# Hybrid attention and gMLP step on eight cores: attention outputs transposed by the loads, first output sums as filler, a finer ramp

## The chip, the cores and the metric

The kernel runs on all 8 cores of one Trainium2 chip, one launch per execution. The time is the device time of the slowest core, in microseconds. Even cores (0, 2, 4, 6) have role 0, odd cores role 1; each pair works on one of four sequences. The two roles run different programs that one function, `emit(ctx, role)`, writes out.

## The reference, cut to what matters

One layer on 4 prompts of 4096 frames and 8 running streams of 16 frames, model width 2048:

```python
h = rmsnorm(x, norm_g)
z = h @ w_in            # columns: q | k | v | f | g_A | u | v_B | g_B
out_a = fox_attention(q, k, v, logf) * silu(g_a)       # 8 heads of 128, causal
out_b = gmlp_mix(gelu(u), layernorm(gelu(v_b))) * silu(g_b)   # 8 groups of 128
y = rmsnorm(x + concat([out_a, out_b]) @ w_out, final_g)
```

The results are y, the keys, the values and the log forget gates, for prompts and streams, and the normalised gMLP rows of the streams.

## The kernel before, in words

A core keeps its normalised input H in SBUF in bf16, channels on partitions, and walks through five stages. Role 0 owns blocks 0 to 19 of its sequence (a block is 128 frames). Role 1 owns blocks 20 to 31 and one stream block of 32 rows, and computes K and V of blocks 0 to 19 for itself once more.

1. **Ramp** (to about 100 us). A *unit* is a pair of blocks. For each unit `n` the list `ramp` (L535) names the steps: `G` scales the unit's x by the norm's gains into H (VectorE and ScalarE, L390 and L392), `S` squares (ScalarE L400, GpSimd L401), `T` ends the tree of sums (VectorE L408, L409), `R` lets TensorE add over the partitions and ScalarE make 1/rms (L420 to L423), `X m` loads the x of unit m, and `K n q` multiplies the unit with the key weights of heads 2q and 2q+1 (`k_mm`) into one PSUM bank; `k_out` (L460) evacuates a bank when its unit has its `R`. The weights `wk`, one tile a head, come over GpSimd's DMA queue, the first three units of x over SP's. The order of the list is the order on every engine.
2. **V, layer norm of gMLP** and the rest of K (to about 460 us).
3. **gMLP** (to about 750 us): `c_chunk` and `mixing`; its products go to the scratch tensor `oT_s`, rows 8 to 15, channels first.
4. **Attention** (about 750 to 1236 us). Heads one after another; in a head the query tiles T (512 queries) from the last to the first; in a tile one *unit* per block of keys: `e_S(i)` is one 128x512 score matmul, then an exp on ScalarE (L1117), a mask on GpSimd on the diagonal (L1120); `e_PV(i-3)` multiplies three units later with V (up to four matmuls of 129 columns). Role 0 has 60 units a head, 480 in all. After a tile's last unit `fin` (L1173, L1176) divides by the sum and multiplies with the gate, into a tile `og`, queries on partitions. Three units later `tr` (L1189 to L1194) lets TensorE transpose it (four transposes of 128x128 into the bank `ob`, L1190), VectorE copies it (L1192), and SP stores it to `oT_s`.
   Between the units TensorE gets *filler*: `qga(h)` computes the queries (`q_item`) and gates (`g_item`, L977 to L984) of the coming tiles. Each step of a generator yields its cost in ns; `due` lists by which unit how much must be done; `fill(i)` raises its target by the steepest of these demands and steps until it is reached. The last demand is everything by unit 474. An item's last step counts 56 whatever it is.
   `wo_load` brings the 16 tiles of `w_out` over GpSimd's queue as memory comes free, mostly in head 7. `o_load` brings a group of four output blocks (16 tiles of 128 KB) from `oT_s` to SBUF over SP's queue.
5. **Output** (about 1236 us to the end). For each of the 20 blocks 64 matmuls of 512 columns (16 channel tiles k times four column groups cg) into four PSUM banks, the order of k in `korder` = 8 to 15, 0 to 7; VectorE adds x (L1332), ScalarE sums squares, VectorE scales (L1340), SP stores y. At each fourth block `o_load` fetches the group after. The last block goes cg by cg, with short evacuations (L1305 to L1325) and four stores.

```python
def fill(i):
    while due and due[0][1] <= filler["target"]:
        due.pop(0)
    if due:
        filler["target"] += max((c - filler["target"]) / max(at - i, 1) for at, c in due)
    ...
    while filler["gen"] is not None and filler["done"] < filler["target"] and ...:
        step()

def icost(it):
    return (tilesP[it[1]][1] / 2.4 + 3) * KC if it[0] == "q" else 56 * KC * (4 if it[1] < NT else 1)
```

Of the kernel before, what the change touches and what calls it, by code (L numbers as in the profile page):

```python
# [51 lines left out]
class Eng:  # L52
# [156 lines left out]
def build_program(only_role=None):  # L209
# [8 lines left out]
    def dscr(name, shape, dt=BF16):  # L218
# [18 lines left out]
        oT_s=dscr("oT_s", [KC, 128, N_HEAD_BLOCKS * 128]))  # L237
# [24 lines left out]
def emit(ctx, role):  # L262
# [28 lines left out]
    def load(q, out, in_, res, part=False, reads=()):  # L291
        q.dma(out, in_, dsem(res.name + "_p") if q is POOL else dsem_of(res), reads=reads, writes=[] if part else [res], pwrites=[res] if part else [])
# [86 lines left out]
    def g_mul(n):  # L379
# [4 lines left out]
        for a0, cnt in ([(0, 1), (1, 1)] if n == 0 else [(0, na)]):  # L384
# [52 lines left out]
    def k_mm(n, heads):  # L437
        u = units_n[n]
        hv, rh = h_of(n)
        bank, w, rows = next_bank(), u["w"], u["rows"]  # L440
        parts = [(a, 1) for a in range(u["na"])] if n == 0 and heads[0] == 0 else [(0, u["na"])]
        for a, cnt in parts:
            for hi_, h in enumerate(heads):
                o = hi_ * w + a * rows
                for k in range(KC):
                    mmop(PSB[bank][:, o:o + cnt * rows], WK[h][:, k, :], hv[:, k, a * rows:(a + cnt) * rows], k == 0, k == KC - 1,
                         rh[a:a + cnt] + [WK[h].r], bank, k == 0 and o == 0, k == KC - 1 and hi_ == len(heads) - 1 and a + cnt == u["na"])
        return n, heads, bank
# [81 lines left out]
    for h in range(2, 8):  # L530
# [4 lines left out]
    ramp = [("G", 0), ("S", 0), ("K", 0, 0), ("T", 0), ("G", 1), ("S", 1), ("X", 3), ("K", 0, 1), ("K", 1, 0), ("R", 0), ("K", 1, 1),  # L535
# [3 lines left out]
    normed, wait = set(), []  # L539
    for e in ramp:  # L540
        what, n = e[:2]
        if what == "G":
            g_mul(n)
# [14 lines left out]
        elif what == "X":  # L558
            x_load(n)
        elif what == "R":  # L560
            rms(n)
            normed.add(n)
        else:
            wait.append(k_mm(n, [2 * e[2], 2 * e[2] + 1]))
# [205 lines left out]
    def cum_gen():  # L770
# [7 lines left out]
        nbt = A.alloc("nbt", [3, 256], F32)  # L778
# [117 lines left out]
    def mixing(gi, ti):  # L896
# [20 lines left out]
        store(SP, io["oT_s"][8 + gi, :, c0:c0 + n], o[:, 0:n], o.r, R_oT[8 + gi][ti])  # L917
# [9 lines left out]
    A.free(*(Ub + Gb + t1))  # L927
# [12 lines left out]
    for T in torder:  # L940
        items += [("q", ti) for ti in TQ[T][::-1] if ("q", ti) not in items] + [("g", T)]
        if smp and T == torder[0]:
            items.append(("g", NT))

# [69 lines left out]
    while (0, "g", torder[0]) not in done:  # L1014
        next(lead)
# [5 lines left out]
    og = [A.alloc("og%d" % i, [4, 128], BF16, hi=True) for i in range(2)]  # L1021
# [22 lines left out]
    def wo_load(n):  # L1044
        for _ in range(n):
            k = wo_next["k"]
            if k >= KC or not A.gaps(D * 2):
                return
            wo[k] = A.alloc("wo%d" % k, [D], BF16)
            load(POOL, wo[k][:, :], io["wout"][k], wo[k].r)  # L1050
            wo_next["k"] += 1

    oT, xr, fgt = [], [], []
# [5 lines left out]
    def o_load(gp, ks):  # L1059
        if gp < len(fgroups):  # L1060
# [3 lines left out]
            for k in ks:  # L1064
                t.res[k].dsem = dsem("oTg%d%s" % (gp % 2, "ab"[k == 7]))
                load(SP, t[:, k, 0:n], io["oT_s"][k, :, c0:c0 + n], t.res[k], reads=[R_oT[k][gi]])
# [32 lines left out]
    pending = []  # L1099
# [62 lines left out]
    def fin(i):  # L1162
# [3 lines left out]
        z = u["tid"] % 2  # L1166
        o, rc = og[z], rec[z]
        need((h, "g", T))
        s = ost[u["tid"] % 3]
        if u["kind"] == "blk":  # L1170
# [9 lines left out]
            nq, rows, c0, n = 4, 128, T * 512, 512  # L1180
        else:
# [43 lines left out]
    due.append((len(units) - 6, cum))  # L1225
# [209 lines left out]
```

How the kernel before makes its waits and increments, by code:

```python
    def _wait(self, ev):  # L60
        sem, val = ev
        if sem is self.sem and self.is_pe:
            return
        if self.seen.get(id(sem), 0) >= val:
            return
        self.eng.wait_ge(sem, val)
        self.seen[id(sem)] = val
# [34 lines left out]
    def op(self, fn, reads=(), writes=(), pwrites=(), sig=True):  # L102
        self._deps(reads, writes, pwrites)
        ins = fn()
        if sig:
            ins.then_inc(self.sem, 1)
            self.cnt += 1
            ev = (self.sem, self.cnt)
        else:
            ev = (self.sem, self.cnt + 1)
        self._update(ev, reads, writes, pwrites)
        return ev
# [1 line left out]
    def dma(self, out, in_, dsem, reads=(), writes=(), pwrites=()):  # L114
        self._deps(reads, writes, pwrites)
        self.eng.dma_start(out=out, in_=in_).then_inc(dsem.sem, 16)
        dsem.cnt += 16
        ev = (dsem.sem, dsem.cnt)
        self._update(ev, reads, writes, pwrites)
        return ev
```

The softmax here doesn't subtract the row's maximum and nothing guards it: scores larger than these inputs give would overflow.

## Time and profile before

| | us |
|---|---|
| median of 3 runs (lowest, highest) | 1529.27 (1529.13, 1530.7) |
| the profiled execution | 1526.34 |
| its span, even cores (role 0) | 1522.6 |
| its spans, odd cores (role 1) | 1500.7 to 1502.7 |
| TensorE busy on core 0 | 1478.3 |
| VectorE, ScalarE, GpSimd busy | 582.1, 608.4, 155.0 |

The span runs from the first to the last instruction of the slowest core; the execution's own time is 3.7 us more. A busy TensorE means that some matmul was in flight, not that it ran at its peak. All times within the span below are of core 0, role 0.

### The profile page before, as it was taken

Reading aid. Unit: us, or ns where it says so; the run is one execution under the profiler, and the core shown is the slowest. Engines: PE = TensorE matmul, PEld = TensorE weight load, DVE = VectorE, ACT = ScalarE, POOL = GpSimd, SP = SyncE. Lnnn points to the kernel's source line nnn. Section 1 sums busy time; section 2 is a strip of 40 time slices with the busy share of each in tenths; the row PEclk is TensorE's granted clock in tenths of the full one; section 3 lists DMA queues with packets and bytes.
Section 4 is the critical chain, followed back from the end, with each engine's and each line's share of the span. In section 5 each row is a group of like instructions: output and inputs, shape, how many; then the busy total and the mean of one; then the engine's idle time right before and its main releaser. Section 6 shows DMA issues by size and latency. Waiting matters only on the chain.

```text
span 1522.6 us, 30070 instructions; the slowest of 8 cores (1500.7 to 1522.6 us)
## 1 busy us (share of the span) xinstructions
PE 1478.3 (97%) x11216; PEld 907.6 (60%) x11216; DVE 582.1 (38%) x1143; ACT 608.4 (40%) x1051; POOL 155.0 (10%) x279
## 2 busy tenths in 40 slices
PE   4999999999999999999999999999999989999997
PEld 3886877854444444444577767777777754444443
DVE  2340222214455655555523333233233333333334
ACT  3322423136662111111366666666666641111112
POOL 4310111210000000000002111112011200000000
PEclk9999999999999999999999999999999999999999
DMA  9993335750003222222516245133340975654643
GB/s 248 241 242 106 128 132 148 164 142 1 1 1 59 48 58 49 49 45 46 81 20 90 40 74 78 37 50 53 45 63 12 191 196 165 201 195 159 221 147 132
DMA packets 86886, 158.13 MB, mean 104 GB/s; under 512 B 28368, under 2 KB 68944, under 8 KB 78544
## 3 DMA queue, kind: packets, MB, share of 16 engines
q0 software_dynamic: 34096, 48.53, 20.9%
q1 hardware_dynamic: 50624, 92.91, 18.4%
q10 hardware_dynamic: 2016, 14.68, 2.8%
q8 instruction: 94, 1.54, 0.4%
q14 instruction: 56, 0.46, 0.1%
HBM read 152.12 MB, written 52.51 MB: 134 GB/s over the span
## 4 chain that ended last, share of the span: by engine, by line
PE 95%; DMA 2%; DVE 1%; issue 1%; ACT 1%; POOL 0%; POOLq 0%; DVEq 0%; ACTq 0%
PE psb L304 94%; DMA arena<-wk 2%; PE psb L1190 1%; DVE arena L1176 0%; ACT arena L1117 0%; POOL arena L116 0%; DVE arena L977 0%; DVE arena L982 0%; POOLq L253 0%; ACT arena L981 0%; DVE arena L1173 0%; DVE arena L1192 0%; ACT arena L1319 0%; ACT arena L1307 0%; DVE arena L1305 0%
## 5 line engine op out<-in xcount | busy, mean ns | idle before, releaser
L304 PE MATMUL psb<-arena 128*128 128x512 bf16 (+5 forms) x11056 | 1475.0, 296 | 33.4 <-DMA arena<-wk 24.3
L304 PEld LDWEIGHTS psb<-arena 128*128 128x128 bf16 x11056 | 900.1, 99 | 602.9 <-issue 50.7
L1117 ACT ACTIVATE arena<-psb,arena 128x512 bf16<-128x512 f32 x480 | 298.8, 632 | 133.9 <-PE psb L304 127.5
L1337 ACT ACTIVATE arena<-arena 128x2048 bf16<-128x2048 f32 x19 | 36.3, 1910 | 224.7 <-DVE arena L1332 224.7
L874 DVE TENSOR_TENSOR arena<-psb,arena 128x512 f32<-128x512 f32 x80 | 55.2, 691 | 97.5 <-PE psb L304 96.0
L1332 DVE TENSOR_TENSOR arena<-psb,arena 128x512 f32<-128x512 f32 x76 | 47.2, 682 | 109.8 <-PE psb L304 109.8
L1120 POOL TENSOR_SCALAR_AFFINE_SELECT arena<-arena 128x128 bf16<-128x128 bf16 x160 | 49.1, 308 | 360.1 <-ACT arena L1117 359.7
L497 ACT ACTIVATE arena<-psb,arena 128x384 f32<-128x384 f32 (+1 forms) x60 | 30.3, 544 | 121.3 <-PE psb L304 106.7
L977 DVE TENSOR_TENSOR arena<-psb,arena 128x512 f32<-128x512 f32 x40 | 27.6, 691 | 120.5 <-PE psb L304 120.5
L891 ACT ACTIVATE arena<-arena 128x512 f32<-128x512 f32 x40 | 25.2, 631 | 117.3 <-DVE arena L874 114.5
L887 ACT ACTIVATE arena<-arena 128x512 bf16<-128x512 f32 x40 | 25.1, 629 | 107.8 <-DVE arena L874 107.7
L401 POOL TENSOR_TENSOR arena<-arena 128x1024 f32<-128x1024 f32 x20 | 46.6, 2352 | 209.4 <-ACT arena L400 209.4
L460 DVE TENSOR_TENSOR arena<-psb,arena 128x512 f32<-128x512 f32 x40 | 26.5, 688 | 101.6 <-PE psb L304 50.6
L1176 DVE SCALAR_TENSOR_TENSOR arena<-psb,arena 128x128 bf16<-128x128 f32 x160 | 56.0, 350 | 17.7 <-DVE arena L1173 1.3
L956 DVE TENSOR_TENSOR arena<-psb,arena 128x512 bf16<-128x512 f32 x40 | 27.6, 689 | 81.4 <-PE psb L304 81.4
L400 ACT ACTIVATE arena<-arena 128x2048 f32<-128x2048 f32 x20 | 37.1, 1901 | 40.7 <-DVE arena L390 40.7
L484 DVE SCALAR_TENSOR_TENSOR arena<-psb,arena 128x8 f32<-128x8 f32 x20 | 4.5, 225 | 114.9 <-PE psb L304 114.9
L1340 DVE SCALAR_TENSOR_TENSOR arena<-arena 128x2048 f32<-128x2048 f32 x19 | 44.7, 2351 | 2.4 <-DVE arena L1339 0.6
L982 DVE SCALAR_TENSOR_TENSOR arena<-arena 128x512 bf16<-128x512 f32 x40 | 27.7, 692 | 33.3 <-ACT arena L981 33.3
L981 ACT ACTIVATE arena<-arena 128x512 f32<-128x512 f32 x40 | 25.2, 630 | 33.3 <-DVE arena L977 33.3
L1192 DVE COPY arena<-psb 128x512 bf16<-128x512 bf16 x40 | 17.0, 424 | 50.9 <-PE psb L1190 48.5
L723 ACT ACTIVATE arena<-psb,arena 128x512 f32<-128x512 f32 x40 | 27.1, 683 | 20.0 <-PE psb L304 18.5
(81 smaller groups left out, 468.6 us busy)
## 6 DMA issues: line engine op xcount, KB each, us to landing
arena<-xn SPq DMA_DIRECT2D x20, 1024.0 KB, 7.3
y<-arena SPq DMA_DIRECT2D x19, 1024.0 KB, 4.8
arena<-xT ACTq DMA_DIRECT2D x14, 1024.0 KB, 10.2
kT<-arena SPq DMA_DIRECT2D x40, 256.0 KB, 9.8
oT_s<-arena SPq DMA_DIRECT2D x80, 128.0 KB, 1.8
arena<-oT_s SPq DMA_DIRECT2D x80, 128.0 KB, 4.7
arena<-wout POOLq DMA_DIRECT2D x16, 512.0 KB, 22.2
vo<-arena SPq DMA_DIRECT2D x40, 192.0 KB, 2.4
```

The costliest lines, as they stand in the source:

```text
L304: PE.op(lambda: mm(out, lhsT, rhs, start=start, stop=stop, **kw), reads=reads, writes=[PSR[bank]] if first else [], pwrites=[] if first el ...
L400: ACT.op(lambda: act.activation(out=x, in_=x, func=AF.Square), reads=[t.res[a]], writes=[t.res[a]])
L401: POOL.op(lambda: g.tensor_tensor(out=x[:, 0:8, :], in0=x[:, 0:8, :], in1=x[:, 8:16, :], op=ALU.add), reads=[t.res[a]], writes=[t.res[a]])
L497: ACT.op(lambda: act.activation(out=o, in_=src, func=AF.Copy, scale=rc), reads=[PSR[bk[c]], rr], writes=[dst.r] if first else [], pwrites= ...
L874: DVE.op(lambda: v.tensor_tensor(out=z[:, 0:n], in0=PSB[b][:, 0:n], in1=rbw[:, c0:c0 + n], op=ALU.mult), reads=[PSR[b]] + rbw.res, writes= ...
L982: DVE.op(lambda: v.scalar_tensor_tensor(out=GAh[p][0:rows, j0:j0 + cnt, :].rearrange("p j c -> p (j c)"), in0=th[0:rows, 0:n], scalar=1.0, ...
L1117: ACT.op(lambda: act.activation(out=P[:, off:512], in_=PSB[b][:, off:512], func=AF.Exp, scale=SCALE, bias=nb[:, T, j, h:h + 1]), reads=[PS ...
L1120: POOL.op(lambda: g.affine_select(out=P[:, off:off + 128], in_=P[:, off:off + 128], pattern=[[1, 128]], compare_op=ALU.is_ge, fill=0.0, ba ...
L1176: DVE.op(lambda c=c, q=q, ps=ps: v.scalar_tensor_tensor(out=o[:, 2 * c + q, :], in0=ps[:, q, 0:128], scalar=rc[:, 2 * c + q:2 * c + q + 1] ...
L1332: DVE.op(lambda cg=cg, b=b: v.tensor_tensor(out=yb[p][q, cg * 512:(cg + 1) * 512], in0=PSB[b][q, :], in1=xr[p][q, cg * 512:(cg + 1) * 512] ...
L1337: ACT.op(lambda: act.activation(out=junk[q, :], in_=yb[p][q, :], func=AF.Square, accum_out=ss), reads=[yb[p].r], writes=[junk.r, R_ss[p]])
L1340: DVE.op(lambda: v.scalar_tensor_tensor(out=yb[p][q, :], in0=yb[p][q, :], scalar=rs, in1=fgt[0][q, :], op0=ALU.mult, op1=ALU.mult), reads= ...
```

## The change

- **Transposes.** `fin` no longer queues `tr`: it stores the tile as it is, queries first, to a new scratch tensor `o_s` (rows of 128 elements, 256 bytes). `o_load` fetches the eight attention tiles of a group with `dma_start_transpose` on SP, the eight gMLP tiles as before (from `mT_s`). TensorE's transposes, VectorE's copies and the list `pending` are gone; `og` has three buffers.
- **Spread loads.** The gMLP tiles of the first output group are loaded when attention begins, and each head's tile right behind its store.
- **Output sums as filler.** Behind the last `qga` the generator `out_ahead` goes through 15 of the 16 k of the first output block for as many column groups as filler has banks (two in role 0, one in role 1), if the weights are there. They are due by unit 479. The weights come in `korder`, and `ring[0]`, `ring[1]` are freed early in head 7.
- **Order of the filler.** A gate item now stands behind the next tile's query item; the lead before attention computes two query items instead of one query and one gate item.
- **Ramp.** K goes in quarters (one head, one block) where weights arrive; `R` and `G` move ahead of the evacuations; `S` and `X` come later.
- **Last block.** Five column groups, the last two of 256; the first two stores go over ScalarE's queue.

```diff
-    ramp = [("G", 0), ("S", 0), ("K", 0, 0), ("T", 0), ("G", 1), ("S", 1), ("X", 3), ("K", 0, 1), ("K", 1, 0), ("R", 0), ("K", 1, 1),
-            ("T", 1), ("G", 2), ("S", 2), ("X", 4), ("K", 0, 2), ("K", 1, 2), ("K", 2, 0), ("R", 1), ("K", 2, 1), ("K", 2, 2),
-            ("T", 2), ("G", 3), ("S", 3), ("K", 0, 3), ...
+    ramp = [("G", 0, [(0, 1), (1, 1)]), ("S", 0), ("K", 0, 0, [(0, 0, 1)]), ("G", 1, [(0, 1)]), ("T", 0), ("G", 1, [(1, 1)]), ("S", 1), ("X", 3),
+            ("K", 0, 0, [(1, 0, 1), (0, 1, 1), (1, 1, 1)]), ("K", 0, 1, [(0, 0, 2)]), ("K", 1, 0, [(0, 0, 1), (1, 0, 1)]), ("K", 1, 1, [(0, 0, 1)]),
+            ("K", 0, 1, [(1, 0, 2)]), ("K", 1, 1, [(1, 0, 1)]), ("K", 1, 0, [(0, 1, 1), (1, 1, 1)]), ("K", 1, 1, [(0, 1, 1), (1, 1, 1)]),
+            ("T", 1), ("G", 2), ("R", 0), ("K", 0, 2), ("K", 1, 2), ("R", 1), ("S", 2), ("X", 4), ("K", 2, 0), ("K", 2, 1), ("K", 2, 2),
+            ("T", 2), ("G", 3), ("R", 2), ("S", 3), ("K", 0, 3), ...
...
+        if i > 0:
+            items.append(("g", torder[i - 1]))
...
-                load(SP, t[:, k, 0:n], io["oT_s"][k, :, c0:c0 + n], t.res[k], reads=[R_oT[k][gi]])
+                src = io["o_s"][k, c0:c0 + n, :] if k < 8 else io["mT_s"][k - 8, :, c0:c0 + n]
+                load(SP, t[:, k, 0:n], src, t.res[k], reads=[R_oT[k][gi]], tr=k < 8)
...
-        def tr():
-            b = ob
-            for q in range(nq):
-                PE.op(lambda q=q: nc.tensor.transpose(psb16[b][:, q * rows:(q + 1) * rows], o[0:rows, q, :], ident[0:rows, 0:rows]),
-            ...
-            DVE.op(lambda: v.tensor_copy(out=s[:, 0:n], in_=psb16[b][:, 0:n]), reads=[PSR[b]], writes=[s.r])
-            store(SP, io["oT_s"][h, :, c0:c0 + n], s[:, 0:n], s.r, R_oT[h][T])
+            store(SP, io["o_s"][h, T * 512:(T + 1) * 512, :].rearrange("(c q) d -> q c d", c=4), o[:, :, :], o.r, R_oT[h][T])
+        if T == torder[0]:
+            o_load(0, [h])
...
+    def out_ahead():
+        for k in korder[:-1]:
+            if wo[k] is None:
+                return
+            for cg in range(len(fbank["list"])):
+                pre.append((k, cg))
+                mmop(PSB[obank[cg]][:, :], oT[0][:, k, ...], wo[k][:, cg * 512:(cg + 1) * 512], k == korder[0], False, ...)
+                yield 216
...
-    due.append((len(units) - 6, cum))
+    due += [(len(units) - 6, cum), (len(units) - 1, cum + 216 * 15 * len(fbank["list"]))]
...
-                A.free(KTh[0], Vh[0], Qh[0], GAh[0])
+                A.free(KTh[0], Vh[0], Qh[0], GAh[0], ring[0], ring[1])
...
-        kcg = [(k, cg) for cg in range(4) for k in korder] if last else [(k, cg) for k in korder for cg in range(4)]
+        cgs = [(512 * i, 512) for i in range(4)] if not last else [(0, 512), (512, 512), (1024, 512), (1536, 256), (1792, 256)]
+        kcg = [(k, cg) for cg in range(5) for k in korder] if last else [(k, cg) for k in korder for cg in range(4)]
...
-                store(SP, dst[:, c4], yb[p][q, c4], R_q[cg])
+                store(ACT if cg < 2 else SP, dst[:, c4], yb[p][q, c4], R_q[cg])
```

## Rows read from the trace of the kernel before

**Rows 1.** The page: busy time by engine, and the chain that ended last.
```profile
PE 1478.3 (97%) x11216; PEld 907.6 (60%) x11216; DVE 582.1 (38%) x1143; ACT 608.4 (40%) x1051; POOL 155.0 (10%) x279
...
PE 95%; DMA 2%; DVE 1%; issue 1%; ACT 1%; POOL 0%; POOLq 0%; DVEq 0%; ACTq 0%
```
**Rows 2.** Spans of the cores, one of role 1.
```profile
core 1: 1500.7 us, clock 0.995
```
**Rows 3.** Attention as a window: length, busy by engine, granted clock, DMA share, GB/s.
```profile
740.00:1250.00 510.00, 496.35 (x5516) 363.12 (x5611) 174.74 (x413) 322.80 (x524) 77.34 (x204) 1.00 0.42 75
```
**Rows 4.** Waits of TensorE over the span: total us, times, longest.
```profile
PE psb L304 <- DMA arena<-wk: 24.1, 5, 13.1
PE psb L304 <- ACT arena L1117: 4.7, 9, 1.2
PE psb L1190 <- DVE arena L1176: 2.0, 3, 1.1
...
PE psb L304 <- DVE arena L1192: 0.7, 1, 0.7
```
**Rows 5.** Lines by form, the transposes: busy us, mean ns, idle before.
```profile
L1190 PE MATMUL psb<-arena 128*128 128x128 bf16 x160 | 15.4, 219 | 2.0 <-DVE arena L1176 2.0
```
**Rows 6.** Timeline of TensorE around one tile's transposes: start, length.
```profile
793.84 0.39 PE L1190 MATMUL psb<-arena 128*128 128x128 bf16 x4
794.06 11.97 PE L304 MATMUL psb<-arena 128*128 128x128 bf16 x135
```
**Rows 7.** End of attention: last gate (timeline), exps behind it (by line), the window.
```profile
1223.29 0.69 DVE L977 TENSOR_TENSOR arena<-psb,arena 128x512 f32<-128x512 f32 x1 [0.79 <-PE psb L304]
...
L1117 ACT ACTIVATE arena<-psb,arena x18: 367/626/688, 1222.8 to 1234.4; 128x512 bf16<-128x512 f32 x9, 128x384 bf16<-128x384 f32 x3, 128x256 bf16<-128x256 f32 x3, 128x128 bf16<-128x128 f32 x3
...
1223.50:1236.30 12.80, 9.23 (x85) 6.03 (x84) 5.38 (x16) 9.58 (x19) 3.50 (x12) 1.00 0.77 196
```
**Rows 8.** Output weights in head 7, by tile: issues on GpSimd's queue, landing.
```profile
L116 POOL DMA_DIRECT2D arena<-wout x12: 528/558/592, 1186.2 to 1202.5; - x12
...
DMA to landing us min/median/max: 11.6/23.7/29.6
```
**Rows 9.** Last block (timeline), its last stores, and 256-column operations (by line).
```profile
1513.81 0.69 DVE L1305 TENSOR_TENSOR arena<-psb,arena 128x512 f32<-128x512 f32 x1
1514.60 0.63 ACT L1307 ACTIVATE arena<-arena 128x512 bf16<-128x512 f32 x1 [1.68 <-DVE arena L1305]
...
1517.04 2.08 SPq L116 DMA_DIRECT2D y<-arena  x4
...
L409 DVE TENSOR_TENSOR arena<-arena 128x256 f32<-128x256 f32 x10 | 4.3, 425 | 1.0
L422 ACT ACTIVATE arena<-arena 128x256 f32<-128x256 f32 x10 | 4.2, 417 | 0.9
```
**Rows 10.** Ramp: timeline of TensorE, with the idle time before.
```profile
25.00 1.91 PE L304 MATMUL psb<-arena 128*128 128x256 bf16 x16 [1.56 <-DMA arena<-wk]
31.45 13.99 PE L304 MATMUL psb<-arena 128*128 128x256 bf16 x102 [4.53 <-DMA arena<-wk]
46.93 13.29 PE L304 MATMUL psb<-arena 128*128 128x256 bf16 x119 [1.49 <-DMA arena<-wk]
```
**Rows 11.** Ramp as windows, columns as in rows 3.
```profile
31.40:36.00 4.60, 4.55 (x22) 3.20 (x23) 0.00 (x0) 0.31 (x1) 3.30 (x2) 0.50 1.01 274
36.00:45.40 9.40, 9.40 (x82) 8.07 (x80) 3.92 (x7) 3.29 (x9) 0.00 (x0) 0.96 0.98 251
```
**Rows 12.** Output stage: landing of oT_s loads (by tile), two groups' issues, SP's queue.
```profile
DMA to landing us min/median/max: 1.7/4.7/6.9
...
1300.93 10.09 SPq L116 DMA_DIRECT2D arena<-oT_s  x16
...
1356.18 9.82 SPq L116 DMA_DIRECT2D arena<-oT_s  x16
...
q1 hardware_dynamic: 50624, 92.91, 18.4%
```

More of the change, by code:

```diff
@@ L383, in g_mul @@
         hv, rh = h_of(n)
-        for a0, cnt in ([(0, 1), (1, 1)] if n == 0 else [(0, na)]):
+        for a0, cnt in parts or [(0, na)]:
             x, rx, rd = t[:, a0:a0 + cnt, :, 0:rows], t.res[a0:a0 + cnt], rh[a0:a0 + cnt]
@@ L435, in next_bank, with k_mm @@
         return b
-    def k_mm(n, heads):
+    def k_mm(n, heads, rec=None, parts=None):
         u = units_n[n]
         hv, rh = h_of(n)
[L440 to L448, printed above, removed]
+        w, rows = u["w"], u["rows"]
+        new = rec is None
+        rec = rec or (n, heads, next_bank())
+        bank = rec[2]
+        for i, (hi_, a, cnt) in enumerate(parts or [(hi_, 0, u["na"]) for hi_ in range(len(heads))]):
+            o = hi_ * w + a * rows
+            for k in range(KC):
+                mmop(PSB[bank][:, o:o + cnt * rows], WK[heads[hi_]][:, k, :], hv[:, k, a * rows:(a + cnt) * rows], k == 0, k == KC - 1,
+                     rh[a:a + cnt] + [WK[heads[hi_]].r], bank, new and k == 0 and i == 0, k == KC - 1)
+        return rec
     def k_out(rec):
@@ L563, in emit @@
         else:
-            wait.append(k_mm(n, [2 * e[2], 2 * e[2] + 1]))
+            part = e[3] if len(e) > 3 else [(0, 0, 2), (1, 0, 2)]
+            rec, got = count.get((n, e[2]), (None, 0))
+            rec, got = k_mm(n, [2 * e[2], 2 * e[2] + 1], rec, part), got + sum(p[2] for p in part)
+            count[n, e[2]] = rec, got
+            if got == 4:
+                wait.append(rec)
         for r_ in [r_ for r_ in wait if r_[0] in normed]:
@@ L939, in emit @@
     items, done = [], set()
-    for T in torder:
-        items += [("q", ti) for ti in TQ[T][::-1] if ("q", ti) not in items] + [("g", T)]
-        if smp and T == torder[0]:
+    for i, T in enumerate(torder):
+        items += [("q", ti) for ti in TQ[T][::-1] if ("q", ti) not in items]
+        if i > 0:
+            items.append(("g", torder[i - 1]))
+        if smp and i == 1:
             items.append(("g", NT))
+    items.append(("g", torder[-1]))
     def q_item(h, ti):
@@ L1013, in emit @@
     fbank["list"] = [6, 7, (cb["n"] + 2) % 6, (cb["n"] + 3) % 6]
-    while (0, "g", torder[0]) not in done:
+    while (0,) + items[len(TQ[torder[0]])] not in done:
         next(lead)
@@ L1020, in emit @@
     Pb = [A.alloc("Pb%d" % i, [512], BF16, hi=True) for i in range(NP)]
-    og = [A.alloc("og%d" % i, [4, 128], BF16, hi=True) for i in range(2)]
+    og = [A.alloc("og%d" % i, [4, 128], BF16, hi=True) for i in range(3)]
     rec = [A.alloc("rec%d" % i, [4], F32, hi=True) for i in range(2)]
@@ L1045, in wo_load @@
         for _ in range(n):
-            k = wo_next["k"]
-            if k >= KC or not A.gaps(D * 2):
+            if wo_next["k"] >= KC or not A.gaps(D * 2):
                 return
+            k = korder[wo_next["k"]]
             wo[k] = A.alloc("wo%d" % k, [D], BF16)
@@ L1208, in fgen @@
             yield from qga(h)
+        yield from out_ahead()
+    pre = []
+    def out_ahead():
[4 more added lines that the diff above has]
+                pre.append((k, cg))
+                mmop(PSB[obank[cg]][:, :], oT[0][:, k, (border[0] % 4) * 128:(border[0] % 4 + 1) * 128], wo[k][:, cg * 512:(cg + 1) * 512],
+                     k == korder[0], False, [oT[0].res[k], wo[k].r], obank[cg], k == korder[0], True)
+                yield 216
     def icost(it):
@@ L1300, in emit @@
         if last:
-            R_q = [Res("yq%d" % i) for i in range(4)]
-            for cg in range(4):
-                b = 4 * p + cg
-                c4 = slice(cg * 512, (cg + 1) * 512)
-                DVE.op(lambda: v.tensor_tensor(out=yb[p][q, c4], in0=PSB[b][q, :], in1=xr[p][q, c4], op=ALU.add),
+            R_q = [Res("yq%d" % i) for i in range(5)]
+            for cg, (g0, w) in enumerate(cgs):
+                b = obank[(4 * p + cg) % 8]
+                c4 = slice(g0, g0 + w)
+                DVE.op(lambda: v.tensor_tensor(out=yb[p][q, c4], in0=PSB[b][q, 0:w], in1=xr[p][q, c4], op=ALU.add),
                        reads=[PSR[b], xr[p].r], writes=[R_q[cg]] + ([yb[p].r] if cg == 0 else []), pwrites=[] if cg == 0 else [yb[p].r])
```

65 lines of the change are left out of this document (27 added, 38 removed), and 5 rows, old and new, of the table ramp.

## The prediction

> **What bounds the kernel now.** I read the page's busy times and its chain first: TensorE is busy 97% of the span and makes up 95% of the chain [rows 1], VectorE and ScalarE are at 40% and below. Then the cores: role 1 ends 21.9 us before role 0 [rows 2], so the time is role 0's, and nothing that only role 1 gains counts. Then attention: of 510 us TensorE is busy 496.4, ScalarE, which makes the exps, 322.8 [rows 3]. Filler keeps TensorE the bound there. Then TensorE's waits [rows 4]: the large one is for the key weights in the ramp; in attention 4.7 us for exps, 2.0 of the transposes for VectorE's `fin`, 0.7 for the copy of the last tile. The sum is made against the profiled execution, 1526.3 us (span 1522.6 and 3.7 around it); the median of the runs shown, 1529.3, is 2.9 higher, and I move both by the same amount.
>
> **1. Transposes off TensorE.** 160 are removed. They are busy 15.4 us, 219 ns each [rows 5], but they overlap with what follows: four start at 793.84 and the next matmul at 794.06 [rows 6], so a tile costs 0.22 us of TensorE's order and 40 tiles 8.8 us. Above, all 15.4 could count; below, nothing, if ScalarE set the pace, but its 63% in rows 3 excludes that for most tiles. I take 8.8, the start-to-start time, as that is what the next matmul waits. The two waits that hang on them go with them: 2.0 + 0.7 = 2.7 us. The Trainium skill, "TensorE: Matmul & The Clock Gate", section "Part 4: PE-mode transpose", gives about 275 ns for a transpose in a kernel's context; by that the term would be 44 us and the time 1482, but here the trace disagrees: 55 ns from one to the next (as a mechanism of this kernel it is rival F). VectorE's 40 copies cost nothing now and give nothing. What is late next is the transposing load.
>
> **2. The transposing loads.** `fin` stores 128 KB as before, in rows of 256 bytes; nobody waits on TensorE, and the three `og` buffers leave at least two tiles, over 8 units of about a microsecond, to land. SP then waits for that store before it issues the load of the same tile, once a head; behind it stands only the next tile's store, 16 units later. In the output stage a group of 16 loads has the time of four blocks: 1356.18 - 1300.93 = 55.2 us [rows 12]. Plain ones take SP 10 us to issue and land within 1.7 to 6.9, median 4.7. The trace has no transposing load. Below, it lands as the fastest plain one, 1.7 us; above, it moves two bytes at a time: 65,536 pieces at the queue's mean per packet (18.4% of 16 x 1522.6 us over 50,624 packets = 88 ns [rows 12]) on 16 engines, 360 us. I take 5 us, the median's size, because one instruction on the same queue names the whole tile, so it is nearest to that row: eight take 40 us even one behind the other, under 55.2, and are used only in the second half of a block's order of k. While they hold SP, the y store and the x load behind them come up to 40 us late; x is needed two blocks (27.6 us) after, so with 7 us of landing VectorE's addition slips by about (40 + 7) - 41 = 6 us, 8 us ahead of the reuse of its banks. Cost 0; without that cover, 8 us per group for each microsecond above 6.9 a load (rival B). The Trainium skill, "VectorE: DVE Perf Modes", section "The three transpose paths", gives 1309 ns for 128x128 by the DMA crossbar; an estimate from it is 5.2 us a load, 42 a group: by that page this term stays 0 and B falls out. No run here shows it yet.
>
> **3. Output sums as filler.** By the planner's own costs a query item counts (512/2.4 + 3) x 16 = 3.46 us and a gate item 3.58, 281.8 us in all, 274.9 without the lead; what the generators really yield is less, since an item's last step counts 56 ns: 268.5. So filler runs dry early. In the trace the last gate is evacuated at 1223.29, and 18 exps run from then on; in 1223.5 to 1236.3 TensorE is idle 12.80 - 9.23 = 3.57 us [rows 7]. The change adds 15 x 2 matmuls, 6.5 us, due by unit 479: the target now rises by (274.9 + 6.5)/479 = 0.587 us a unit, and 268.8 + 6.5 us last until unit 468, where before they ended at 462. A third of the 18 bare units is covered, so 3.57 x 6/18 = 1.2 us is gained; the matmuls themselves are only moved. Bounds: 0 to 3.57. They need 15 of 16 weight tiles. Of the twelve loaded in head 7, the last lands at up to 1202.5 + 29.6 us [rows 8], and the reordered gates free H some six units later; but two ring buffers come free at once, and 2 MB of output tiles have been loaded before. I take the weights as just in time; the loss if not is a rival.
>
> **4. Tail.** The last sum waits for 256 columns instead of 512: VectorE 0.43 for 0.69, ScalarE 0.42 for 0.63 [rows 9], 0.5 us. Four stores on SP took 2.08 us; with two on ScalarE about 0.5 of that goes. Gain 1.0, bounds 0 and 1.6.
>
> **5. Ramp.** TensorE stands still for weights at 25.00, 31.45 and 46.93, and never after [rows 10]; in this stretch the DMA engines are full (share 0.98 to 1.01 [rows 11]). The fifth tile (head 4) lands at 46.9, and everything behind it waits for it in either order. The quarters fill the gap of 4.5 us before 31.45: 16 matmuls of 256 columns and three sixteens of 128 are 4.8 us from 25.00. Behind 31.45 seven sixteens of 128 columns are left, about 6.5 us, so they end at 38 instead of 45.4. Nothing is won: TensorE now waits 9 us before 46.9 where it waited 1.5. And after such a pause it runs slower: behind the 4.5 us one, 22 matmuls took 4.60 us at a granted clock of 0.50, 1.2 GHz, then 82 took 9.40 at 0.96, close to 2.4 GHz [rows 11]. At the second rate the 22 take 2.5, so the slow start cost 2.1 us, until now in slack. Moved behind 46.9 it is on the path: +2.1. On the other side two stores of keys (0.5 MB, 2 us of the DMA engines at 251 GB/s) leave the window before 46.9, because `R 0` now stands behind `G 2`, which waits for the third x; of that the weights' queue, one of three, gets some 0.6. Net +1.5, bounds -1.5 and +2.3. `S 2`, `X 4` and the value weights are issued some 10 us later, where TensorE has 30 us or more of K before it needs them: 0, and if that cover fails, a wait for x in the fifth unit.
>
> Everything else at 0: the new place of the gates (still due two units before use), the lead (the same 7 us), allocations. **Sum:** -8.8 - 2.7 - 1.2 - 1.0 + 1.5 = -12.2: 1514.1 for the profiled execution, 1517 for the median. Role 1 sheds 104 transposes and stays ahead.
>
> **Rivals.** *A, forecast*: 1517, its own range 1514 to 1521; chance 0.60.
> *B, slower*: the transposing loads set the pace of the output stage. The point is 55.2/8 = 6.9 us a load. At twice the plain median, 9.4, a group takes 75 us, 20 too long, four times: 1517 + 80 = 1597. For it speaks that no row shows such a load; against it that one would have to take longer than the slowest plain one of 64. Chance 0.06.
> *C*: the time freed is not on the path, because units are paced by ScalarE: only the waits, filler and tail count, -2.7 - 1.2 - 1.0 + 1.5 = -3.4, 1526. For it: TensorE's 4.7 us of waits for exps; against it: 63%. Chance 0.09.
> *D*: the fifth weight comes early enough that the clock holds (term 5 at -1.5), and the short gaps around tiles close: 13.65 us of idle in rows 3 less 7.4 named in rows 4 leaves 6, half of it 3. 1517 - 6 = 1511. Chance 0.10.
> *E*: the output weights are late, and TensorE, in order, stands before them with scores queued behind. Two tiles later by six units is 6 us: 1523. For it: landing times of up to 29.6 us; against it: less traffic. Chance 0.10.
> *F*: a transpose costs its whole 219 ns: 160 x 219 ns = 35 us, 26 more: 1491. Rows 6 speak against it. Chance 0.03.
> *G*, the change doesn't do what it says: `out_ahead` returns at once because a weight tile has no room yet; 1518. Chance 0.02.
>
> **The numbers.** A measurement of this kernel tells about 0.2%, 3.1 us, from no change. Faster by more: A, D, E, F, G and half of C, 0.89; within: the rest of C, 0.05; slower: B, 0.06. The range 1511 to 1523 takes in A, D, E and G, 0.82; it leaves out B, C and F.
>
> **What would show it.** No L1190 and L1192; next matmul behind a tile without the 0.22 us; about 12 us less between 750 and 1237. Transposing loads that land in 2 to 6 us and no wait of TensorE for them; one would prove B. In the ramp one wait before the fifth weight of about 9 us at 47, and a granted clock of 0.5 behind it. Thirty matmuls of 512 columns before the last exp, fewer than 18 exps behind the last filler. It is wrong if attention is not some 11 us shorter, or if a new wait stands in the output stage.

## The result and the profile after

The changed kernel takes 1519.39 us (median of 1518.79, 1519.39 and 1523.55; before 1529.27). The ratio is 0.994, 95% interval [0.9912, 0.9969]: faster by 0.6%, and inside the range. A fourth, disturbed execution of 7076.91 us is left out; with it the median is 1521.47, which the expectations below start from. The sum of the parts was -12.2 us; the profiled execution, 1518.79, has -7.5, and the span of its slowest core went from 1522.6 to 1514.3, -8.3.

The page (of core 4, as are the views below unless said otherwise): busy time, and the chain by engine.
```profile
PE 1469.4 (97%) x11136; PEld 902.6 (60%) x11136; DVE 570.1 (38%) x1115; ACT 609.9 (40%) x1059; POOL 153.8 (10%) x279
...
PE 94%; DMA 3%; ACT 1%; issue 1%; POOL 1%; DVE 0%; POOLq 0%; ACTq 0%; DVEq 0%
```
Against [rows 1] TensorE has 8.9 us less work and 80 records less (160 transposes gone; 64 matmuls more by the quarters, 16 by the split columns). The bound is unchanged.

The cores: one of role 1 beside the slowest of role 0.
```profile
core 1: 1491.8 us, clock 0.994
core 4: 1514.3 us, clock 0.996
```
Role 1 stays ahead ([rows 2]: 21.9 us, now 22.5).

The waits of TensorE over the span: total us, times, longest.
```profile
PE psb L304 <- DMA arena<-wk: 27.8, 6, 13.3
PE psb L304 <- ACT arena L1132: 4.3, 11, 0.7
...
PE psb L304 <- DVE arena L991: 0.7, 1, 0.7
```
The waits of the transposes in [rows 4] are gone, no wait for a transposing load or an output weight stands in their place, and the wait for the key weights has grown from 24.1 to 27.8.

Three rows, by line, cut the span into stages: the last V evacuation ends the ramp and the value projections, the last gate of the gMLP stands ahead of attention, the x additions are the output stage (first and last start).
```profile
L499 ACT ACTIVATE arena<-psb,arena x60: 463/574/583, 111.9 to 323.8; 128x384 f32<-128x384 f32 x40, 128x256 f32<-128x256 f32 x20
...
L902 ACT ACTIVATE arena<-arena x40: 629/631/633, 485.4 to 749.9; 128x512 f32<-128x512 f32 x40
...
L1345 DVE TENSOR_TENSOR arena<-psb,arena x76: 678/680/693, 1243.0 to 1493.5; 128x512 f32<-128x512 f32 x76
```
The same three rows of core 4 before.
```profile
L497 ACT ACTIVATE arena<-psb,arena x60: 463/574/582, 107.3 to 319.1; 128x384 f32<-128x384 f32 x40, 128x256 f32<-128x256 f32 x20
...
L891 ACT ACTIVATE arena<-arena x40: 629/631/632, 480.6 to 745.1; 128x512 f32<-128x512 f32 x40
...
L1332 DVE TENSOR_TENSOR arena<-psb,arena x76: 678/680/692, 1250.9 to 1501.3; 128x512 f32<-128x512 f32 x76
```
The ramp ends 4.7 later on this core, 3.5 in the mean of the four cores of role 0. From the last gMLP gate to the first x addition it was 505.8 and is 493.1: -12.7. The output stage is 250.4 and 250.5. The last addition to the end of the span was 21.3 and is 20.8: -0.5. With 0.1 between the first two rows these make -8.3. **So attention gave all that was forecast for it, and the ramp took back over a third.**

Attention as a window, columns as in [rows 3].
```profile
740.00:1250.00 510.00, 503.29 (x5511) 360.10 (x5510) 166.37 (x387) 327.55 (x529) 76.47 (x204) 1.00 0.46 74
```
TensorE is idle 6.7 us of these 510 where it was 13.65. And the end of attention, which in [rows 7] had 3.57 us idle of 12.80, has 2.0:
```profile
1224.00:1236.80 12.80, 10.82 (x88) 6.46 (x86) 4.42 (x16) 8.53 (x16) 3.50 (x12) 1.00 0.17 37
```

The transposing loads, by tile in the output stage, and two of their groups on SP's queue.
```profile
L116 SPq DMA_TRANSPOSE arena<-o_s x32: 1122/1262/2398, 1244.1 to 1419.6; - x32
...
DMA to landing us min/median/max: 2.6/4.0/7.5
...
1244.05 10.65 SPq L116 DMA_TRANSPOSE arena<-o_s  x8
1254.79 0.53 SPq L116 DMA_DIRECT2D y<-arena  x1
...
1298.97 10.28 SPq L116 DMA_TRANSPOSE arena<-o_s  x8
```
Each holds SP for 1.26 us, but lands as a plain one does (4.0, [rows 12]: 4.7).

### The profile page after: what moved, and what is told of

It reads as the page before. It is cut to its first block, busy times and chain, and to the rows that moved or that the text cites. A ratio compares the mean times of both kernels' runs of the same rounds, so it can differ in the third digit from the quotient of the medians.

```text
span 1514.3 us, 29871 instructions; the slowest of 8 cores (1485.7 to 1514.3 us)
## 1 busy us (share of the span) xinstructions
PE 1469.4 (97%) x11136; PEld 902.6 (60%) x11136; DVE 570.1 (38%) x1115; ACT 609.9 (40%) x1059; POOL 153.8 (10%) x279
## 4 chain that ended last, share of the span: by engine, by line
PE 94%; DMA 3%; ACT 1%; issue 1%; POOL 1%; DVE 0%; POOLq 0%; ACTq 0%; DVEq 0%
PE psb L304 94%; DMA arena<-wk 3%; ACT arena L1132 1%; POOL arena L401 0%; POOL arena L116 0%; DVE arena L408 0%; ACT arena L400 0%; POOLq L253 0%; ACT arena L1332 0%; DVE arena L991 0%; ACT arena L1320 0%; ACTq L116 0%; ACT arena L499 0%; POOL arena L524 0%; ACTq L66 0%
## 5 line engine op out<-in xcount | busy, mean ns | idle before, releaser
L304 PE MATMUL psb<-arena 128*128 128x512 bf16 (+6 forms) x11136 | 1469.4, 295 | 36.6 <-DMA arena<-wk 27.8
L304 PEld LDWEIGHTS psb<-arena 128*128 128x128 bf16 (+1 forms) x11136 | 902.6, 99 | 603.1 <-issue 50.9
L885 DVE TENSOR_TENSOR arena<-psb,arena 128x512 f32<-128x512 f32 x80 | 55.2, 691 | 97.5 <-PE psb L304 96.0
L390 DVE TENSOR_SCALAR arena<-arena 128x256 bf16<-128x256 f32 (+1 forms) x120 | 32.5, 347 | 17.8 <-DMA arena<-xT 17.8
```

What stands on the lines that cost most here:

```text
L304: PE.op(lambda: mm(out, lhsT, rhs, start=start, stop=stop, **kw), reads=reads, writes=[PSR[bank]] if first else [], pwrites=[] if first el ...
L390: DVE.op(lambda: v.tensor_scalar(out=o, in0=x[:, :, k, :], scalar1=gcol[:, k:k + 1], scalar2=None, op0=ALU.mult), **kw)
L885: DVE.op(lambda: v.tensor_tensor(out=z[:, 0:n], in0=PSB[b][:, 0:n], in1=rbw[:, c0:c0 + n], op=ALU.mult), reads=[PSR[b]] + rbw.res, writes= ...
```

## The experiments

Times, ratios to the kernel before on the same chip, and stages from the profiles; the means are over the four cores of role 0. The "gate" is the end of the last wait for a key weight, at 46.9 to 50 us, for head 5.

```
kernel               us       ratio [95%]              gate   last V evacuation  gMLP to x addition
before               1529.27                           46.93  319.1              505.8
changed              1519.39  0.994  [0.9912, 0.9969]  47.98  322.6              493.0
first chip
 e1_old_ramp         -                                 48.26  320.4              493.6
 e2_new_ramp_only    1537.58  1.0048 [1.0033, 1.0063]  48.88  324.5              505.6
 e3_no_ahead         1521.42  0.9956 [0.9939, 0.9972]  49.11  324.0              494.6
 e4_warm             1519.06  0.9931 [0.9918, 0.9944]  48.95  322.0              493.9
second chip
 e5_changed_again    1518.09  0.9943 [0.993, 0.9955]   47.86  322.3              493.5
 e6_old_order        1517.51  0.9929 [0.9915, 0.9942]  47.35  320.4              493.2
 e8_tail             1516.60  0.9926 [0.9912, 0.9939]  47.54  320.9              493.2
third chip
 e10_head4_first     1519.10  0.9936 [0.9922, 0.995]   -      322.0              492.9
 e11_square_early    1524.29  0.997  [0.9958, 0.9982]  -      323.2              492.8
 e12_new_ramp_tail   1518.48  0.9933 [0.9919, 0.9947]  -      322.0              492.8
```

### Ramp and attention apart

**e1_old_ramp**: the change with the order of before in the ramp; **e2_new_ramp_only**: before with the new ramp.
```diff
-    ramp = [("G", 0, [(0, 1), (1, 1)]), ("S", 0), ("K", 0, 0, [(0, 0, 1)]), ("G", 1, [(0, 1)]), ("T", 0),
...
+    ramp = [("G", 0, [(0, 1), (1, 1)]), ("S", 0), ("K", 0, 0, [(0, 0, 1), (1, 0, 1), (0, 1, 1), (1, 1, 1)]), ("T", 0), ("G", 1),
...
```


> The changed kernel with the old list of ramp steps; all else as changed. My theory now: the new ramp takes back 3 to 4.5 us, because TensorE runs at the lower clock behind longer waits for weights. Then this runs at 1517 to 1518.5, 3 to 4.5 under the changed kernel's 1521.5 (ratio to before 0.992), the first evacuation of a V unit comes at 107.2 as before (110 to 112 with the change), and core spans of role 0 differ by less than 1 us. Rival: the ramp is neutral and the 4 us that the forecast missed were lost in attention or the output stage, to the transposing loads or the filler: 1521 to 1522.

> The kernel before with the new ramp alone. My theory: slower than before by 2 to 5 us, 1531.5 to 1534.5, first V evacuation at 110 to 112, attention and output as long as before. Rival (ramp neutral): 1529 to 1530, first V evacuation at 107.

e1 has only two times that count, 1517.45 and 1519.96, too few for a ratio; its stages say that attention keeps its -12.2 without the new ramp. Its first V evacuation comes at 108.1 to 108.8, later than the 107.2 expected. e2 is 0.5% slower than before, more than expected: attention is as before (505.6), the ramp 5.4 longer in the mean and 7.6 on the slowest core, which sets the time. So these are two independent parts of opposite sign.

**e3_no_ahead**: no output sums as filler.
```diff
-        yield from out_ahead()
...
-    due += [(len(units) - 6, cum), (len(units) - 1, cum + 216 * 15 * len(fbank["list"]))]
+    due.append((len(units) - 6, cum))
```


> The changed kernel without the output sums as filler (the first output block is summed whole behind attention). My theory: the 30 matmuls were only moved, and a third of the bare units covered, so this is 0.5 to 1.2 us slower than the changed kernel, 1522 to 1522.7. Rival 1: they fill all idle time at the end of attention, 3.6 us: 1525. Rival 2: waiting for the gate's bank and for weights eats it: 1521.5 or less.

Without the filler, gMLP to x addition is 494.6 (493.8 to 496.1 by core); in the runs that keep it the means are 492.8 to 493.9. So the filler is worth 0.7 to 1.8 us (forecast 1.2), and not clear of the spread of the cores: in e3's core 0, at 496.1, the granted clock falls to 0.50 around 1233, and without that core the mean is 494.1. Against before, e3, with only the transposes and their waits gone, is 11.2 shorter here (forecast 8.8 + 2.7 = 11.5).

**e6_old_order**: e1, and the gates and their lead as before.
```diff
-    while (0,) + items[len(TQ[torder[0]])] not in done:
+    while (0, "g", torder[0]) not in done:
...
```


> The changed kernel with the old ramp, the old order of gates and queries and the old lead. Theory: the new order and lead give 1.3 us (from the last gMLP evacuation to the first exp 6.7 us with the change, 8.0 before), so this is 1.3 slower than the kernel with the old ramp alone, and that interval is 8.0 again. Rival: the interval moved with the ramp or by the order of VectorE's work, not by the lead: 6.7 stays.

The gap from the last gMLP gate to the first exp is 8.0 us as before instead of 6.8, and gMLP to x addition is still 493.2 (the changed kernel: 493.0 and 493.5): what the shorter lead gains is given back inside attention. The kernel isn't the 1.3 us slower that was expected; the cost of 0 for order and lead holds.

### The ramp

First, what the gate is. The ramp of before, core 0 to 48.6 us, by form.
```profile
L304 PE MATMUL psb<-arena 128*128 128x256 bf16 x128 | 17.2, 300 | 7.6 <-DMA arena<-wk 7.6
L304 PE MATMUL psb<-arena 128*128 128x128 bf16 x64 | 6.9, 304 | 16.5 <-DMA arena<-wk 16.5
```
The 64 of 128 columns are heads 0 and 1 of the first unit. The 128 are 16 behind the wait at 25.00, 96 behind 31.45 (102 records less six norm sums, [rows 10]) and 16 behind 46.93. Heads 0 to 3 of two units leave 96 of 256 columns, so 16 more ran before 46.93: head 4 of the first unit. What TensorE waits for at 46.93 is head 5, the sixth tile; the prediction took it for the fifth.

After, core 4, the timeline of TensorE.
```profile
25.16 4.59 PE L304 MATMUL psb<-arena 128*128 128x256 bf16 x64 [1.36 <-DMA arena<-wk]
33.16 7.20 PE L304 MATMUL psb<-arena 128*128 128x256 bf16 x102 [3.41 <-DMA arena<-wk]
42.21 1.91 PE L304 MATMUL psb<-arena 128*128 128x256 bf16 x16 [1.85 <-DMA arena<-wk]
48.60 18.23 PE L304 MATMUL psb<-arena 128*128 128x256 bf16 x150 [4.48 <-DMA arena<-wk]
67.00 3.21 PE L304 MATMUL psb<-arena 128*128 128x256 f32 x26 [0.17 <-DVE arena L390]
```
And its windows there, columns as in [rows 3].
```profile
49.00:50.00 1.00, 1.00 (x6) 0.72 (x5) 0.00 (x0) 0.00 (x0) 0.00 (x0) 0.50 0.91 147
...
52.00:53.00 1.00, 1.00 (x12) 0.89 (x10) 0.69 (x1) 0.00 (x0) 0.00 (x0) 1.00 0.97 213
```
Head 4 is done early, head 5 opens the gate at 48.60 instead of 46.93, with the same work behind it: +1.7. Behind the gate the granted clock is 0.50, the lower of its two levels (1.2 GHz), until about 52 us; then it is 1.00 (2.4 GHz).

**e4_warm**: the change with 14 and 36 matmuls, whose result nobody reads, ahead of heads 4 and 5 of the first unit.
```diff
-("R", 0), ("K", 0, 2), ("K", 1, 2), ("R", 1)
+("R", 0), ("W", 14), ("K", 0, 2, [(0, 0, 2)]), ("W", 36), ("K", 0, 2, [(1, 0, 2)]), ("K", 1, 2), ("R", 1)
...
```


> The changed kernel with 14 + 36 matmuls of 256 columns into an idle bank while TensorE waits for the fifth and the sixth tile of key weights (they add work whose result nobody reads; 5.4 us of it, within the 6.3 us of waits). Theory (the clock): the granted clock stays near 1.0 from 40 to 60 us, the 144 matmuls behind the sixth tile take 16.4 us instead of 18.2, and the time falls by 1.5 to 3 us to 1519. Rival (the late weights themselves cost the time, the clock is a by-product): the clock rises but the first V evacuation stays at 110 to 112, and the time at 1521.5. Second rival: the filling work itself delays the weights' matmuls: 1522 to 1523.

Its timeline of TensorE on core 6:
```profile
48.57 16.68 PE L304 MATMUL psb<-arena 128*128 128x256 bf16 x150 [0.52 <-DMA arena<-wk]
```
The same 150 matmuls take 16.68 at a granted clock of 1.00, so the clock cost 1.55 of the 18.23 above; the time, 1519.06, is what this theory expected. The last V evacuation comes 2.0 us before that of e3, which has the change's ramp on the same chip and a nearly equal gate (49.11, here 48.95). Now take the gate from the last V evacuation: what is left is 272.1 to 272.2 on all cores of before and e1, with the old ramp and a clock that holds; e4 has 272.5 on three cores (on the fourth a norm sum waits 1.8 us for the tree of the fifth unit); the changed kernel 273.6 to 275.4. The old ramp can lose the clock too: of the eight even cores of e6 and e8, which have it, five waited 2.8 to 3.3 us for the sixth tile, had 0.50 behind it and are left with 273.8 to 273.9; three waited 1.7 to 2.2, kept 1.00 and have 272.1 to 272.2. Two of them, e6's cores 0 and 4, as windows:
```profile
48.60:67.00 18.40, 18.40 (x155) 15.96 (x154) 7.45 (x17) 5.25 (x12) 5.72 (x4) 0.91 1.03 238
...
48.60:67.00 18.40, 18.40 (x169) 16.55 (x168) 7.46 (x17) 7.71 (x12) 5.72 (x4) 1.00 1.04 242
```
That is the whole ramp: **when the sixth tile lands, plus what the clock and later waits cost behind it**.

**e10_head4_first**: TensorE works on heads for which weights are there, instead of standing.
```diff
-("R", 0), ("K", 0, 2), ("K", 1, 2), ("R", 1), ("S", 2), ("X", 4), ("K", 2, 0), ("K", 2, 1), ("K", 2, 2),
+("R", 0), ("K", 0, 2, [(0, 0, 2)]), ("K", 1, 2, [(0, 0, 2)]), ("K", 2, 0), ("K", 0, 2, [(1, 0, 2)]), ("K", 1, 2, [(1, 0, 2)]), ("R", 1), ("S", 2), ("X", 4), ("K", 2, 1), ("K", 2, 2),
```


> The changed kernel with one step of its ramp moved: while the sixth key weight tile (head 5) is still on its way, TensorE computes head 4 of the second unit and heads 0 and 1 of the third unit, instead of standing and then running at half the clock. Theory (the missing microseconds of the ramp are the wait for the sixth tile and the half clock behind it): the wait on that tile falls from 4.5 to 6 us to under 1 us, the granted clock stays at or near 1.00 between 45 and 55 us, the last V evacuation starts at 318 to 319.5 (322.1, 322.8, 321.7, 322.5 in the repeated run of the change), and the time is 3 to 4.5 us under the change's, 1514 to 1515.5, ratio about 0.991 to 0.992. Rival (the ramp is late for a cause behind 60 us: the sums and squares of later units, loads issued late): the wait goes, but the last V evacuation stays at 321 to 323 and the time at 1517 to 1519.

The wait goes, the gain doesn't come, as its rival said: 322.0, and 1519.10. Core 0, TensorE and then VectorE:
```profile
33.45 27.13 PE L304 MATMUL psb<-arena 128*128 128x256 bf16 x268 [2.75 <-DMA arena<-wk]
64.24 70.99 PE L304 MATMUL psb<-arena 128*128 128x256 f32 x544 [3.66 <-DVE arena L390]
...
61.43 2.02 DVE L408 TENSOR_TENSOR arena<-arena 128x1024 f32<-128x1024 f32 x2 [4.82 <-POOL arena L401]
63.56 0.42 DVE L409 TENSOR_TENSOR arena<-arena 128x256 f32<-128x256 f32 x1
63.90 2.71 DVE L390 TENSOR_SCALAR arena<-arena 128x256 bf16<-128x256 f32 x10
```
TensorE runs through without a gap for head 5, and then waits 3.66 us for the scaled x of the fourth unit, which stands on VectorE behind the tree of the third, which waits for GpSimd's sums, which wait for the squares that the change moved behind `R 1`. Before, this tree began at 59.5. In the changed kernel the same wait is 0.17 (at 67.00 above): the moved squares are hidden by the gate with nothing to spare. The lower clock follows the new wait (0.66 in the mean of 65 to 70 us).

**e11_square_early**: e10 with `S 2` and `X 4` back ahead of these heads.
```diff
-("R", 0), ("K", 0, 2, [(0, 0, 2)]),
+("R", 0), ("S", 2), ("X", 4), ("K", 0, 2, [(0, 0, 2)]),
...
-("R", 1), ("S", 2), ("X", 4), ("K", 2, 1), ("K", 2, 2),
+("R", 1), ("K", 2, 1), ("K", 2, 2),
```


> The run before with the squares of the third unit and the load of the fifth unit's x put back to where they stood before the change, ahead of the key projections of the fifth and sixth heads. Theory: where a core showed a wait of 1.0 to 1.8 us of the last norm sum on the tree of the fifth unit, it is gone on all four cores; the last V evacuation is at or below the run before by 0 to 1.8 us, 317 to 319. Rival: the squares on ScalarE now hold back the first evacuations (3.3 to 4.3 us of ScalarE), so banks come free later and TensorE waits; the last V evacuation is later than in the run before by 1 to 3 us.

Neither theory holds, and the kernel is 5 us slower than e10. The last V evacuation is 321.2, 323.0, 318.4 and 330.1. Core 4 has no wait behind 42.67 us and beats even before's 319.1; cores 0 and 2 wait 2.8 us for a tree; core 6, VectorE and then TensorE:
```profile
85.41 0.69 DVE L462 TENSOR_TENSOR arena<-psb,arena 128x512 f32<-128x512 f32 x1 [9.55 <-DMA kT<-arena]
...
87.33 2.01 DVE L408 TENSOR_TENSOR arena<-arena 128x1024 f32<-128x1024 f32 x2
...
89.79 2.45 DVE L390 TENSOR_SCALAR arena<-arena 128x256 bf16<-128x256 f32 x9
...
90.13 45.16 PE L304 MATMUL psb<-arena 128*128 128x256 f32 x326 [10.62 <-DVE arena L390]
```
The evacuation of a key bank waits 9.55 us for a store of keys to leave its staging buffer, and in VectorE's order the tree, the scaling and TensorE stand behind it. Stores of keys that are issued up to 100 us land after a median of 18 to 20 us in this run, 11 to 15 in the changed kernel. With x and value weights asked for earlier, they share DMA engines that are full (0.99 and more between 40 and 70 us on this core); that this is the cause is argued, not shown, as they land late on core 4 too. The six times lie between 1524.16 and 1524.52, and in each the slowest even core has a span of 1519.6 to 1520.0, be it core 0, 2, 4 or 6: the stall belongs to the order, not to one core.

### The loads and the tail

**e7_loads_x6** and **e9_loads_x3**: each transposing load of the second and later groups issued six and three times, the additional ones into spare tiles.
```diff
+                for x in range(5 if k < 8 and gp > 0 else 0):
+                    load(SP, dm[x * 8 + k][:, 0:n], src, dm[x * 8 + k].r, reads=[R_oT[k][gi]], tr=True)
...
```


> The changed kernel with each transposing load of the output stage issued six times, five of them into spare tiles that nobody reads. A load holds SP 1.3 to 1.5 us in a group of eight, so a group holds SP 48 x 1.4 + 5 = 72 us where it has 55.2. Theory (rival B's mechanism, with its price): the output stage becomes SP's, about 17 us longer per group, 1521 + 50 to 70. Other theory: the loads overlap each other more when many are under way (0.6 us each) and nothing changes: 1521.

> Each transposing load of the second and later groups issued three times, two of them into spare tiles. SP is held 24 x 1.35 us and the plain loads behind them, some 38 us a group, under the 57.5 us that a group of four blocks takes. Theory (the loads have slack on SP and only the loads of x behind them would be late): an x load slips by up to 22 us, and with one block of lead of about 14.3 us the output stage waits 0 to 8 us a group: 1518 to 1545. Rival (the loads are already at the edge, any more of them delays TensorE by what they add): 3 groups x 22 us, over 1570.

One run each: 1675.33 and 1551.24. SP's queue and TensorE's wait in e7 (core 2):
```profile
1248.71 64.62 SPq L116 DMA_TRANSPOSE arena<-o_s  x48
...
PE psb L304 <- DVE arena L1351: 140.9, 4, 36.3
```
and in e9 (core 0):
```profile
1249.23 33.26 SPq L116 DMA_TRANSPOSE arena<-o_s  x24
...
PE psb L304 <- DVE arena L1351: 17.7, 9, 6.2
```
Neither run does what either of its theories said. Three times lies above the first theory's 1518 to 1545 and under the rival's 1570: the output stage grows by 27 to 33 us, 7 to 8 for each of the four groups that are loaded in it (the expectation counted three). In e7 it grows by 150 to 153 us, 38 a group. In neither does TensorE wait for a transposed tile; in e7 these land after a median of 2.8 us. It waits for the x addition on VectorE, and that for the x loads that stand behind the transposing ones on SP:
```profile
DVE arena L1351 <- DMA arena<-xn: 219.4, 4, 55.9
```
That is e7, core 2. On the two cores above SP is held 32 and 64 us a group, and 7.0 and 38.2 are lost, of which 4.4 and 35.2 are waits of TensorE; behind them the granted clock is 0.50 for a while (e9, core 0, 1355 to 1359 us). A straight line gives 25 us held as the point where the loss begins, 28 where the waits do, and about one us lost for each one more (estimates from two runs); the change holds SP for 10.3 to 10.7.

**e8_tail**: e1, and the third column group goes the way of the last two.
```diff
-                if cg < 3:
+                if cg < 2:
...
```


> The changed kernel with the old ramp, and in the last block the third column group is no longer multiplied ahead by the final gains (it goes with the last two in one operation). Theory: that multiplication stands in VectorE's order ahead of the additions of both 256-column groups, so that the split gained nothing; without it the time from the last matmul to the end of the sums falls from 1.7 to 1.2 us, and the whole tail by 0.3 to 0.5. Together with the old ramp 1516.5 to 1518, 3 to 5 under the changed kernel of this job. Rival: ScalarE's squares in a row set it, and nothing changes in the tail.

The sums end 1.15 us behind the last matmul where the changed kernel has 1.67, but that is not what the edit gives. With the change's tail they end 1.66 to 1.68 behind in the changed kernel and in e5, and 1.30 to 1.32 in e1, e3, e6 and e10 (before: 1.61 to 1.62); in the changed kernel the third product starts after 1.27 us idle, in those four after 0.92, and no row says why. Against e1 the edit takes 0.17 off the sums, and the last scaling on VectorE, which has the third product now, ends 0.1 later. The end of the span comes 8.15 to 8.28 behind the last matmul, and in kernels with the change's tail anywhere from 7.98 to 9.05: what the edit is worth is not shown. 1516.6 lies 1.5 under the change on the same chip, of which the old ramp and the old order (e6) have 0.6; the intervals overlap. **e12_new_ramp_tail** joined e10's ramp to it.

> The ramp of the run with head 4 first joined to the tail in which the third column group goes the way of the last two. If the ramp theory holds it beats the tail variant on the old ramp (1516.6): 1513 to 1515. If the ramp theory falls, 1516 to 1519.

1518.48, ratio 0.9933: no better. **e5_changed_again** is the change itself, for comparison on its chip.

> The changed kernel once more, unedited, beside the next three on one chip. Expected 1521.5 (1519 to 1523.5), ratio 0.994; last V evacuation of role 0 at 322 to 324 against 319 before, from run to run 1 to 2 us apart with the landing of the sixth weight tile. If the chip alone made the difference between this and the kernel with the old ramp, both come out alike.

e8_tail has the lowest time of all, but its interval overlaps with those of the change and of e6.

## Why the prediction was right, and where it was not

**Terms 1 to 3 (transposes, loads, filler), -12.7: right.** Attention became 12.7 shorter on the slowest core, 12.0 to 13.0 in the means of the experiments that keep them. The price of a transpose was its start-to-start time of 55 ns, not the 219 of a row: e3's 11.2, less the 2.7 of the waits, is 53 ns each, and leaves nothing for the copies on VectorE. The loads were taken at 5 us and land in 4.0. Cost 0 held, but the margin was put in the wrong place: rival B counted the time to land, and e7 and e9 show that the time the loads hold SP, ahead of the loads of x, decides, from about 25 us a group on and not from 55.2. The page "VectorE: DVE Perf Modes" of the Trainium skill (section "The three transpose paths") would have made it 5.2 us, an estimate of four times its 1309 ns; the median here is under that, and by either the term is 0. After, the last gate is at 1216.55 and the filler behind it fills TensorE to 1228.5:
```profile
1217.39 11.09 PE L304 MATMUL psb<-arena 128*128 128x512 bf16 x83 [0.73 <-DVE arena L991]
```
The output weights landed in time (7.9 to 28.5 us, no wait for them): E and G are out; so are C and F, by the -12.7.

**Term 5 (ramp), +1.5: this is the step that failed, by its size.** The ramp took 4.7 on the slowest core, 3.5 in the mean, where its bounds were -1.5 and +2.3. The prediction misread one row: the wait at 46.93 is for the sixth tile (head 5), not for the fifth. So its sign for the ramp, one wait of about 9 us, failed: there are two, 1.85 us for the fifth and 4.48 for the sixth. The two parts of the term were "+2.1" for the clock and "-0.6" because stores of keys leave the window before the gate. The clock cost 1.55, as said and where said (e4). But the gate did not come 0.6 earlier. It came 1.7 later on the slowest core, 1.05 in the mean of four; against the old ramp on one chip, 0.3 to 0.9. And behind it stand costs the sum put at 0. The wait for the tree is 0.17 where `S 2` was to have cover to spare. A second fall of the clock, to 0.81, costs about 1.2 us: in these 7 us core 4 starts 56 matmuls, core 0, at 1.00, 67.
```profile
73.50:80.50 7.00, 7.00 (x56) 5.82 (x55) 1.55 (x3) 2.07 (x6) 3.77 (x4) 0.82 1.07 228
...
73.50:80.50 7.00, 7.00 (x67) 6.27 (x65) 3.21 (x4) 1.26 (x4) 2.95 (x3) 1.00 1.06 250
```
So on core 4 it is 1.7 + 1.55 + 0.2 + 1.2 = 4.65 of 4.7. On some cores of other runs `R 4` waits 1.0 to 3.7 us for the tree of the fifth unit; the prediction had named a late x there as what would follow if its cover failed, but putting `X 4` back (e11) did not remove that wait, so its cause isn't shown. Between kernels of one chip the new ramp's last V evacuation is 1.3 to 4.1 later than the old one's. Why the sixth tile lands later stays open: e1, e6 and e8, with the old ramp, have it at 47.35 to 48.26 where before has 46.93, so part of it isn't the ramp's order, and a difference between chips is not ruled out. The cause of the second fall of the clock is open too.

**Term 4 (tail), -1.0: at most half right.** From the last matmul to the end of the span it was 8.9 and is 8.3. That the stores on two queues gave this is not shown: e1 and e6, with the same tail, have 8.7 to 9.05. The 0.5 of the split columns did not come here, and only 0.3 of it in e1, e3, e6 and e10. Columns: start, length, last idle.
```profile
1505.62 0.69 DVE L1323 TENSOR_TENSOR arena<-arena 128x512 f32<-128x512 f32 x1 [1.27 <-ACT arena L1320]
1506.23 0.75 DVE L1318 TENSOR_TENSOR arena<-psb,arena 128x256 f32<-128x256 f32 x2
```
The last matmul ends at 1505.98, but both additions of 256 columns stand behind the product of the third group on VectorE, and the sums end at 1507.65, 1.67 behind the matmul; before it was 1.62.

**The range** held: 1519.39 lies in A's own 1514 to 1521, 2.4 above the forecast. The error is +3.2 in the ramp and +0.5 in the tail on the slowest core. The ramp left the bounds of its own term, and the time stayed inside only because the larger terms beside it came as forecast; this much was luck. D had said that the weights come early and the clock holds: the fifth did come early, but the sixth is the gate.

## What to carry to other kernels

Ahead of a gate that a transfer sets, work done earlier was worth nothing here, and what was moved past it for that purpose lost its cover: name the tile behind each wait by counting the matmuls up to it, and list the waits that come next with their slack. In this ramp, with the DMA engines full, each wait taken away uncovered another (tile, squares, staging buffer); fewer bytes or another order of the transfers was not tried. A DMA that takes the place of a plain one is priced twice, by its landing and by how long it holds the queue that others share.

## What was not expected of the hardware

The granted clock fell a second time, to 0.81, neither of the two levels, on core 4 (74 to 80 us) and on core 6 (73 to 79), though TensorE had been busy for about 25 us. Cores 0 and 2 and e5 have no such fall. A transposing DMA of 128 KB held SP for a median of 1.26 us (plain ones of a group: 0.6), and yet landed as early. Four cores that agreed within 0.1 us in the ramp of before (319.0 to 319.1) spread over 1.1 and 2.0 us in the two profiles of the changed kernel, and with the same ramp over 6.4 in e9 and 7.0 in e7; over 4.3 in e2 and 11.7 in e11. The old ramp spreads too, by 2.2 in e6 and 2.0 in e8, where only some cores lose the clock. As the slowest core sets the time, the spread is paid in full.
